# Two prompt tiles and the samples are routed first, and the V products of four tiles are made in one pass

## What is computed

```python
q = (x @ w_query).reshape(T, 8, 2, 128)
s = einsum('thpd,hpkd->thpk', q, sub_keys)           # 128 scores per head and side
s1, i1 = top_k(s[:, :, 0], 16); s2, i2 = top_k(s[:, :, 1], 16)
top_s, top_pos = top_k(all 256 sums s1[a] + s2[b], 16)
e_idx = (i1 * 128 + i2) at top_pos;  gate = softmax(top_s)
a = gelu(einsum('thkd,td->thk', u_tab[e_idx], x))    # exact gelu
y = einsum('thk,thkd->td', gate * a, v_tab[e_idx])
```

## Time and profile before

| | |
|---|---|
| median of 3 runs | 3245.22 us (3241.13 to 3252.75) |
| profiled execution | 3243.07 us, span 3241.0 us |
| PE busy | 3143.3 us, 97% of the span |
| PE weight load | 2775.6 us, 86% |
| DVE busy | 2379.3 us, 73% |
| ACT busy | 995.1 us, 31% |
| POOL busy | 796.9 us, 25% |
| mean granted TensorE clock | 0.985 of full speed |
| moved by DMA | 754.30 MB, mean 233 GB/s |

### The profile page before, as it was taken

How to read it: one execution, slowest core, us unless ns; L and a number is a source line. 1 busy time by engine, 2 the same in 40 slices (tenths; PEclk the granted TensorE clock), 3 DMA queues, 4 the chain that set the end, 5 groups by cost and what they waited for, 6 DMA issues and landing times. The chain is left out here.

```text
span 3241.0 us, 49377 instructions
## 1 busy us (share of the span) xinstructions
PE 3143.3 (97%) x17258; PEld 2775.6 (86%) x17258; DVE 2379.3 (73%) x5085; ACT 995.1 (31%) x1487; POOL 796.9 (25%) x588
## 2 busy tenths in 40 slices
PE   6999999799999999999999999999999999999999
PEld 4777777578999999999999999977888888888887
DVE  5676555445999768999577777648888888888886
ACT  4323333222222123444222222223333334333333
POOL 0000000001111100000376656534333333433330
PEclk9999999899999999999999999999999999999999
DMA  4111110222221223778999999989999999999993
GB/s 164 41 47 58 55 41 28 92 92 96 72 72 59 69 92 115 241 239 259 334 412 377 369 360 360 353 299 403 364 353 352 357 354 392 383 356 352 353 351 139
DMA packets 324580, 754.30 MB, mean 233 GB/s; under 512 B 22456, under 2 KB 154044, under 8 KB 323312
## 3 DMA queue, kind: packets, MB, share of 16 engines
q1 hardware_dynamic: 145024, 408.29, 34.6%
q0 software_dynamic: 79776, 290.00, 23.7%
q10 hardware_dynamic: 99664, 54.56, 5.7%
HBM read 637.82 MB, written 114.95 MB: 232 GB/s over the span
## 5 line engine op out<-in xcount | busy, mean ns | idle before, releaser
L1251 PE MATMUL u_p<-hn_hi,u_hi 128*128 128x384 f32 x2048 | 699.4, 342 | 7.4 <-PEq L1274 3.7
L1253 PE MATMUL u_p<-hn_hi,u_lo 128*128 128x384 f32 x2048 | 692.9, 338 | 0.0
L1252 PE MATMUL u_p<-hn_lo,u_hi 128*128 128x384 f32 x2048 | 692.6, 338 | 0.0
L1941 POOL DMA_INDIRECT y_ring<-in_peer_v,row_idx x248 | 367.5, 1482 | 624.8 <-DVE yt L2083 574.8
L1745 POOL DMA_INDIRECT s_ring<-in_peer_u,row_idx x264 | 334.8, 1268 | 620.2 <-DVE row_idx L1838 411.7
L1987 PE MATMUL y_p<-v_hi,w_hi 128*128 128x512 f32 x1536 | 474.5, 390 | 10.4 <-DVE w_lo L2074 10.4
L1989 PE MATMUL y_p<-v_lo,w_hi 128*128 128x512 f32 x1536 | 474.2, 390 | 0.0
L1992 PE MATMUL y_p<-v_hi,w_lo 128*128 128x512 f32 x1536 | 473.7, 390 | 0.0
L1251 PEld LDWEIGHTS u_p<-hn_hi,u_hi 128*128 128x128 f32 x2048 | 386.0, 188 | 9.4 <-issue 7.4
L1252 PEld LDWEIGHTS u_p<-hn_lo,u_hi 128*128 128x128 f32 x2048 | 386.2, 189 | 0.0
L1253 PEld LDWEIGHTS u_p<-hn_hi,u_lo 128*128 128x128 f32 x2048 | 386.1, 189 | 0.0
(11 more groups left out here) (350 smaller groups left out, 4694.4 us busy)
## 6 DMA issues: line engine op xcount, KB each, us to landing
u_raw<-in_peer_ut SPq DMA_DIRECT2D x128, 512.0 KB, 7.7
late<-in_peer_v SPq DMA_DIRECT2D x64, 1024.0 KB, 7.4
down_raw<-in_peer_v SPq DMA_DIRECT2D x64, 1024.0 KB, 7.2
act_scratch<-act_tile SPq DMA_DIRECT2D x128, 384.0 KB, 5.7
gate_scratch<-gbuf ACTq DMA_DIRECT2D x6, 4096.0 KB, 16.4
gate_scratch<-late ACTq DMA_DIRECT2D x6, 4096.0 KB, 20.8
late<-act_scratch SPq DMA_DIRECT2D x64, 384.0 KB, 8.6
late<-gate_scratch SPq DMA_DIRECT2D x64, 384.0 KB, 10.3
```

Source lines behind the costliest of these rows:

```text
L1251: mm(b, uh[:, s, k, :], hn_hi[:, k, t], start=(k == 0), stop=False)
L1252: mm(b, uh[:, s, k, :], hn_lo[:, k, t], start=False, stop=False)
L1253: last = mm(b, ul[:, s, k, :], hn_hi[:, k, t], start=False, stop=(k == ND - 1))
L1941: nc.gpsimd.indirect_dma_start(out=ring[:, n % RING, :], out_offset=None, in_=A["peer_v"], in_offset=bass.IndirectOffsetOnAxis(ap=idx[:, N ...
```

## The change

The expert layer gets this order:

1. **First search** (10 blocks): queries (264 columns) and search for tiles 6, 7 and the samples only, one block per head. The low parts of U are on POOL here alone.
2. **First decode** (4 blocks): those tiles. Row numbers are written to `idx` here.
3. **Second search** (88 blocks): 16 sections of 6 and 5 blocks. A section searches three of tiles 0 to 5 for one head (queries of 384 columns, made from a second load of `w_query`). Between the six parts of a search DVE makes a U low part and some dots or adds (`fill_of`): 264 dots in sections 0 to 8, 192 adds of V rows in sections 9 to 15. Sample activations now use two buffers (`hb`), and `yt` holds first the rows for the dots and, once the last dot is done, the rows that are added to.
4. **Second decode** (6 blocks): tiles 0 to 5. Tiles 4 and 5 are not transposed; their expert numbers go to `idx`, together with the place of their activation in `act_scratch`.
5. **Gates** for 8 sub-blocks (512 tokens) with 16 blocks, then 4 blocks alone.
6. **V** in one pass over tiles 0 to 3, 64 pairs of 48 products. Tiles 4 and 5 stay dense in U, but go by rows in V: their activations, one number for each (token, pick), are fetched from `act_scratch` by 256 indexed fetches (`pick`), and 320 rows are fetched and added in all, 64 left of tile 7 and 256 of tiles 4 and 5. How many adds DVE makes after a pair is set by `due`.

The search keeps 64 of the 256 sums, those that can be among the top 16 (`RECTS`), and the decode has nine small chained operations that turn such a position into the two ranks.

The diff, cut to its core:

```diff
-NV1 = 8
-TL = TG // 2
+TV = 4
+GV = NC - TV
+NG2 = GV * P - NG
+TL = TV
-E_TOPK, E_DECODE = 22, 10
+E_K1, E_D1, E_K2, E_D2 = 10, 4, 88, 6
+K2_ADDS = 192
...
+    RECTS = [(0, 1, TOPK, 0), (1, 3, 8, 16), (4, 4, 4, 40), (8, 8, 1, 56)]
+    NCAND = 64
...
+            NSEC = 2 * PH
+            SD = 9
+            FIRST_U = [E0 + 11 * (s // 2) + 6 * (s % 2) for s in range(NSEC + 1)]
+            JOBS = [NDOT * min(s, SD) // SD + K2_ADDS * max(s - SD, 0) // (NSEC - SD) for s in range(NSEC + 1)]
...
+                def sample_row(i):
+                    if i >= 2:
+                        pool.wait_ge(dot_done, NG + i - 1)
+                    elif i == 1:
+                        pool.wait_ge(dot_done, NK)
+                    nc.gpsimd.dma_start(hb[i % 2][:, :], hs_dram[NG + i:NG + i + 1, :].broadcast_to([P, D])
+                                        ).then_inc(hb_in[i % 2], 16)
...
+                    if s == SD - 1:
+                        sp.wait_ge(dot_done, NDOT)
+                        sp.dma_start(yt[:, :, :], x2_dram[DENSE:SEQ, :].rearrange("(t p) d -> p t d", p=P)).then_inc(xt_in, 16)
...
+                for s in range(NSEC):
+                    for i, e in enumerate(range(FIRST_U[s], FIRST_U[s + 1])):
+                        if s + 1 < NSEC and i == 3:
+                            chunk(s + 1)
+                        if s + 1 < NSEC and i == 4:
+                            scores(s + 1)
+                        tile_products(pe, e)
...
+                    def fill(i):
+                        e = FIRST_U[s] + i + 1
+                        if e <= FIRST_U[s + 1]:
+                            u_low(dve, nc.vector, e, e % 2)
+                        a, z = (JOBS[s] + (JOBS[s + 1] - JOBS[s]) * x // 6 for x in (i, i + 1))
+                        for n in range(a, z):
+                            if n < NDOT:
+                                dot(n)
+                            else:
+                                add(n - NDOT)
...
+    KEPT = NG - K2_ADDS
+    NADD = KEPT + NG2
+    FROM = [1, 18, 58]
+    DONE = [0, KEPT, NADD]
...
+        def due(n):
+            for x in range(2):
+                if n <= FROM[x + 1]:
+                    return DONE[x] + (DONE[x + 1] - DONE[x]) * max(n - FROM[x], 0) // (FROM[x + 1] - FROM[x])
+            return NADD
...
+            def pick(c):
+                nc.gpsimd.indirect_dma_start(
+                    out=picked[:, c:c + 1], out_offset=None, in_=acts,
+                    in_offset=bass.IndirectOffsetOnAxis(ap=idx[:, NU + NG2 + c:NU + NG2 + c + 1], axis=0)
+                ).then_inc(act_in[c // SUB], 16)
...
+            for n in range(RING, KEPT + RING):
+                for c in range(2):
+                    pick(2 * (n - RING) + c)
+                row(n)
+            for n in range(KEPT + RING, NADD):
+                c = 2 * KEPT + n - KEPT - RING
+                if c < NG2:
+                    pick(c)
+                row(n)
...
-            for g in range(2):
-                pair(g, 0, 0, first=True)
-                with pe.Fori(0, NP // 2 - 1) as i:
-                    pair(g, 2 * i + 1, 1)
-                    pair(g, 2 * i + 2, 0)
-                pair(g, NP - 1, 1, last=True)
+            pair(0, 0, first=True)
+            with pe.Fori(0, NP // 2 - 1) as i:
+                pair(2 * i + 1, 1)
+                pair(2 * i + 2, 0)
+            pair(NP - 1, 1, last=True)
...
+            for n in range(NP - SLOTS):
+                pair(n, n % SLOTS, n // SLOTS, fresh=(n == 0))
+                adds(n)
```

More of the change, by code:

```diff
@@ new lines, in query_low, with query @@
+    def query_low(dve, n):
+        dve.wait_ge(wqhi_done, n + 1)
+        nc.vector.tensor_tensor(wql[:, :, :], wq[:, :, :], wqh[:, :, :].bitcast(F32),
+                                ALU.subtract).then_inc(wqlo_done, 1)
+    def query(pe, n, b, side, t):
+        if n >= 2:
+            pe.wait_ge(q_out, n - 1)
+        d = slice(side * P, (side + 1) * P)
+        for k in range(ND):
+            nc.tensor.matmul(b, wqh[:, k, d], hn_hi[:, k, t], start=(k == 0), stop=False)
+            nc.tensor.matmul(b, wqh[:, k, d], hn_lo[:, k, t], start=False, stop=False)
+            last = nc.tensor.matmul(b, wql[:, k, d], hn_hi[:, k, t], start=False, stop=(k == ND - 1))
+        last.then_inc(q_done, 1)
@@ L1641, in _ @@
                         a_store(sp, e, p)
-            sp.wait_ge(saved[0], 16 * (NSUB // 2) + 16)
+            with sp.Fori(0, NJ) as j:
+                four(j)
+            for e in range(R0, R0 + 2):
+                tile_in(sp, e)
+            for s in range(2):
+                sp.wait_ge(saved[s], 16 * NJ + 16)
+            for s in range(2):
+                Pair(sem, s, late[:, s * SLOT:(s + 1) * SLOT]).load(sp, A, a_dram, g_dram, s)
+            for e in range(R0 + 2, NK):
+                tile_in(sp, e)
         @block.tensor
@@ L1693, in _ @@
                                  gbuf[s][:, :, :].rearrange("i (q e) t -> i q e t", e=2)).then_inc(saved[s], 16)
+            with act.Fori(0, NJ) as j:
+                two(j)
+            for e in range(R0, NK):
+                tile_out(act, e)
         @block.vector
@@ L1889, in down_phase @@
-def down_phase(nc, A, O, own, sb, ps, sem, x2_dram, g_dram, a_dram, ys, yt, idx, wt, late):
+                            u_low(dve, nc.vector, G0 + 4 * j + 2 * s + n // 4 + 1, (n // 4 + 1) % 2)
+            with dve.Fori(0, NJ) as j:
+                two(j)
+            for e in range(R0 + 1, NK):
+                u_low(dve, nc.vector, e, e % 2)
+def down_phase(nc, A, O, own, sb, ps, sem, x2_dram, g_dram, a_dram, ys, yt, idx, wt, gate_tok, late):
     N = TL * P
@@ L1946, in _ @@
+            for n in range(RING):
+                row(n)
+            for p in range(2):
+                pool.wait_ge(a_out[p], 16 * (NK // 2))
+            for n in range(RING, KEPT + RING):
[6 more added lines that the diff above has]
+                    pick(c)
+                row(n)
         @block.sync
@@ L1973, in _, with pair @@
             mm = nc.tensor.matmul
-            def pair(g, j, s, first=False, last=False):
-                n = NP * g + j
+            def pair(n, s, first=False, last=False):
                 pe.wait_ge(vlo_done, 2 * n + 2)
@@ new lines, in weights, with evacuate @@
+            def weights(t):
+                c = slice((t - TV) * NK, (t - TV + 1) * NK)
+                dve.wait_ge(x2_in, 16)
+                for i in range(c.start // SUB, c.stop // SUB):
+                    dve.wait_ge(act_in[i], 16 * SUB)
+                w = slice(NG + c.start, NG + c.stop)
+                v.tensor_tensor(wt[:, w], picked[:, c], gate_tok[:, w], ALU.mult).then_inc(wt_done, 1)
+                dve.wait_ge(wt_done, t - TV + 1)
+            def evacuate(t):
+                if t == 0:
+                    dve.wait_ge(x_in, 16)
+                dve.wait_ge(tile_done, t + 1)
@@ new lines, in _ @@
+            q = NQ - 1
+            pair(SLOTS * q, 0, q)
+            pair(SLOTS * q + 1, 1, q)
+            mean(slice(TL, NT), len(FIRST))
+            pair(SLOTS * q + 2, 2, q)
+            inverse(slice(TL, NT), 1)
+            pair(SLOTS * q + 3, 3, q)
+            for t in FIRST:
+                scale(t, 1)
+            for t in range(TL):
+                evacuate(t)
+                mean(slice(t, t + 1), len(FIRST) + t + 1)
+                inverse(slice(t, t + 1), t + 2)
+                scale(t, t + 2)
```

1123 lines of the change are left out of this document (550 added, 573 removed).

## The result

| | before | after |
|---|---|---|
| median of 4 runs | 3248.98 us (3241.13 to 3254.18) | 3290.26 us (3284.89 to 3301.98) |
| profiled execution | 3243.07 us | 3285.14 us, span 3283.3 |
| up to 742 us, the mixer | 742 | 742 |
| everything up to V | 1424 us | 1529 us |
| V with start and tail | 1075 us | 1012 us |

The ratio is 1.0127 with a 95% interval of 1.0101 to 1.0152: the kernel became **slower by 1.3%**. The forecast was faster by 0.7%; the measured time lies inside the range that it gave, 3115 to 3320, but on the other side of no change.

The account below looks back on a forecast made before the run. TensorE's products were taken to set the time now, busy 98 to 100% from 742 us on. 3243 + 86 for the stages before V - 108 for V = 3221 us, 3223 on the runs' scale; range 3115 to 3320.

Parts of the forecast that it names:

- First search, first decode, second decode and gates: Four stages before V, forecast at 150, 46, 71 and 237 us.
- The third part of V: Rows 200 to 319 of V: VectorE sets 2.14 us a row, 257 us, with DMA just carrying it at 399 GB/s.
- the prediction's own signs against it: In V: a pick under 0.6 us, GpSimd waiting for the ring early, or TensorE above 90% would disprove that part.
- the one for the second search: Second search: VectorE busy under 88% would prove its forecast of about 1000 us wrong.
- Rival (c): Late in V, DMA binds at 364 GB/s: a pair takes 15.0 us instead of 13.7, kernel 3247; chance 0.09.
- the price of a call in V: In V, GpSimd calls cost 1.36 and 1.42 us each: 192 calls take 261 us, 256 take 364.
- Rival (a): In V, GpSimd's calls cost more: at 1.6 us V takes 1059, the kernel 3313 + 2; chance 0.30.
- the mismatch term of the second search: Second search: VectorE waits 17 us where long TensorE stretches meet its short ones and the other way round.
- VectorE is the bound there: Second search: VectorE's work of 934 us against TensorE's 883, busy 93% or more, stage 1006 us with waits.
- the end of V: After V's last add: six pairs 65 us and tail 8.
- (b): In V, a pick is cheap, 0.7 us with its gap: V 801, the kernel 3055; chance 0.13.
- (d): Second search: fills hide VectorE's waits, so 1006 falls to some 935, the kernel to 3150; chance 0.06.

Follow-up runs that it names:

- a1: The changed kernel without V's 256 fetches of single activations (output differs): 3106.1 us, ratio 0.9546, V 824 us.
- a2: The changed kernel with each add of a fetched row in V on 16 of 1024 columns (output differs): 3257.5 us, ratio 1.0034.
- c2: The changed kernel with 256 instead of 192 adds in the second search and V's rows spread late: 3233.6 us, ratio 0.9937.
- d2: The changed kernel with VectorE in V waiting for four rows, so adds come in bursts of four: 3284.1 us, ratio 1.0106.
- d1: The changed kernel with the 88 low parts of U in the second search back on GpSimd: 3306.4 us, ratio 1.0187.
- b3: The changed kernel with dots and adds of the second search on 16 of 1024 columns (output differs): 3236.3 us, one run.
- b1: The changed kernel with each section's first low part of U ahead of the search's first maxima: 3269.9 us, ratio 1.0063.
- b2: The changed kernel with the eight sample dots spread, one after each 16 dots of tile 7: 3278.2 us, ratio 1.0085.
- c1: The changed kernel with V's adds respread: 64 until pair 24, 136 until pair 53, 120 in pairs 53 to 59: 3233.0 us, ratio 0.9944.
- e1: The three edits of c3 with a later spread: 64 adds until pair 25, 136 until 56, 120 beside 56 to 59: 3189.1 us, ratio 0.9823.
- c3: The changed kernel with the edits of b1, b2 and c1 together: 3200.0 us, ratio 0.9844.

## Why the prediction was wrong, step by step

**The change of stages was read rightly.** First search, first decode, second decode and gates came within 7 us each (147, 39, 75, 235 for 150, 46, 71, 237). Nothing of what TensorE saved on gates was left, as forecast, and V was set by GpSimd for two thirds, with no engine else full. The third part of V, 257 us for its last 120 rows, took 259. Of the prediction's own signs against it, none of those for V came and the one for the second search did, VectorE under 88% (83%). The rate at which DMA binds was right too: 397 GB/s for 259 us, where the earlier trace rows had 403 for 72 us. Rival (c) did not come. The Trainium skill's 358 GB/s per core (DMA: Bandwidth & Descriptors, Specifications) is below what a single working core moves here, and its page HBM Reference (Specifications) says so of a core streaming alone; a1's 406 GB/s for 462 us agrees.

**The step that failed is the price of a call in V**, "1.36 and 1.42 us a call, so 261 and 364 us". It is 275 / 192 = 1.43 and 378 / 256 = 1.48, 28 us more, of the 45 that V took above its sum. The prediction itself had put the point of no gain at 1.44, and had the row for 1.48, 27 calls in 40 us; it set it aside because VectorE would be less busy. VectorE was less busy (57 and 68% against 79%), but that is not what counts. Rival (a) was the right mechanism, at a smaller price than its 1.6. What a call costs hangs on the moment at which it starts. Three calls of the kernel after, and the adds beside them:

```profile
2608.78 1.08 POOL L2080 DMA_INDIRECT y_ring<-in_peer_v,row_idx  x1 [0.30 <-issue]
2610.17 0.94 POOL L2071 DMA_INDIRECT picked_act<-act_scratch,row_idx  x1 [0.30 <-issue]
2611.42 1.65 POOL L2080 DMA_INDIRECT y_ring<-in_peer_v,row_idx  x1 [0.30 <-issue]
```

```profile
2607.76 1.28 DVE L2225 SCALAR_TENSOR_TENSOR y_late<-y_ring,row_weight,y_late 128x1024 f32<-128x1024 f32 x1
2610.97 1.29 DVE L2225 SCALAR_TENSOR_TENSOR y_late<-y_ring,row_weight,y_late 128x1024 f32<-128x1024 f32 x1 [1.92 <-DMA y_ring<-in_peer_v,row_idx]
```

The first call starts when the add has 0.26 us to go and takes 1.08; the second meets none and takes 0.94; the third has 0.84 us of an add ahead of it and takes 1.65. In each the time is what is left of the add, plus 0.82, and never below 0.94. So it is for 413 of the 448 calls, to 0.07 us; nearly all of the others start as the instruction of VectorE begins, and take 0.94 where this would give 2.08. The 182 calls that start within no instruction of two SBUF inputs take 0.95 at most, though the DMA engines are busy for 82 and 83% there; the other 266 take 1.28 in the mean, and that lengthening is 89 us of the 653. All instructions of VectorE that lengthen a call here read two inputs in SBUF; no run sets one of the same length with one input beside the calls, so that it needs two is not shown. The pair's own low parts lengthen calls as well as adds do (a2, c2), and a VectorE that waits for rows makes short separate stretches, each of which can catch a call (d2). The Trainium skill (SBUF — State Buffer, Who interferes with whom) says that the ports which VectorE and GpSimd share are an exclusive lock, and that a VectorE instruction with two SBUF inputs contends with a GpSimd instruction that reads SBUF; the three calls agree. d1 shows it in the other direction, a dot of 3.18 us beside a low part on GpSimd.

**Second, the mismatch term of the second search**, "17 where TensorE's long stretch (a query chunk beside an expert, 16.8) meets a short one of VectorE". VectorE's waits for high parts of U and of the query are 73.0 + 12.1 = 85 us. The other waits were well sized: 10.8 + 15.0 + 6.8 + 13.9 = 46.5 for 9 + 21 + 9 + 16 = 55. With its waits of 131.6 taken off, VectorE's work, with the short gaps between its instructions, is 901 us where the sum had 934, so the forecast had 33 too much work and 60 too little waiting, together the 27. The claim that VectorE is the bound there, at 93%, is wrong as a claim about one engine: with dots and adds of 16 columns (b3), the search still lasts 975. The bound is a chain of two engines with one block of slack; order alone is worth 30 us (b1), the samples' dots 12 (b2) and load 52 for 64 adds (c2).

**Third, the end of V**, 65 + 8 = 73 us for six pairs and the tail. From 3197 us on it was 86: 6 until the weights of the next pair are there, 67 for six pairs (the first, behind a stop of TensorE, took 12.7, the others 10.9), 13 for tile sums, roots and stores. The first eight rows took 14 for 12, and with the 2 of the third part that is V's 45: 2 + 28 + 2 + 13.

Together: -3 - 7 + 27 + 4 - 2 + 45 = 64, and 3221 + 64 = 3285, the profiled execution. The forecast's margin was 22 us; the price of the calls alone used it up, the other two made the kernel slower.

**The rivals that failed.** (b), a cheap call for 4 bytes: its duration is that of 4 KB, 0.94 us. (d), fills that hide VectorE's waits: 132 us of waits stayed, and the search took 1033 us where (d) had some 935.

**What the prediction did not see.** It took the spread of adds over pairs (`due`) as given. With calls as the bound, the pairs beside them are free for TensorE up to its 10.9 us each. The change puts 39 pairs under 653 us of calls and leaves 25 for the stretches where DMA and VectorE are full or nothing is beside them. With 52 there (c1) V falls by 56 us: the sign of the change hangs on a schedule. TensorE's clock says where that time lay: 0.82 of full speed over the 378 us in which TensorE was busy for 70%, a mean between its levels of 1.2 and 2.4 GHz. In e1's second part, with TensorE busy for 87% of it, it is 0.93.

**Still open.** How much of V's gap to the 697 us of TensorE could be had is not shown. Fewer calls for the same picks would be the way; none that does it was tried. In the search, c3 stands 100 us above TensorE's sum of 896, of which load, order, start and end are shown as causes. In its trace TensorE waits 48 us for low parts, and 28 pass between the last product of U and the next stage; what each cause has of the 48 is not shown.

## What to carry to other kernels

Count an engine's calls, not their bytes: an indexed fetch of 4 bytes costs GpSimd what one of 4 KB does, and if the calls set a stage, add to the price what is left, on average, of VectorE's two-input instruction when a call starts, or take it from the busiest row that you have. Where a stage is set by one engine's fixed count of calls, put as much of the other engines' work beside them as will fit, and only then judge the change. Where two engines hand each other work with a slack of one block, neither's sum of busy time is the stage: look for what stands ahead of the handed-over instruction in its engine's order.

## What was not expected of the hardware

- VectorE and GpSimd hold each other up in both directions, and not only at row fetches. A GpSimd call that starts within `v_lo` or `w_lo` takes up to 1.97 us instead of 0.94. A dot that starts within a GpSimd subtraction takes 3.18 instead of 1.23. In d1, giving the low parts to a GpSimd that was busy for 56% made VectorE busy for 69 us more, though it had 107 us less to do.
- With VectorE still for 28 us, 23 calls were issued in c2, 1.22 us each, and in that kernel's first 160 us, VectorE busy for 38%, 1.50. Between these ends the price is set by how many calls start within a two-input instruction and how much of it is left, not by VectorE's busy share as such.

```profile
2512.00:2540.00 28.00, 0.00 (x0) 0.00 (x0) 0.00 (x0) 0.00 (x0) 21.12 (x23) 0.50 0.02 0
```

- The 16 DMA engines stayed at 397 to 406 GB/s for 259 and 462 us, with fetched rows of 4 KB in over half of the bytes. In a2 that pace held a stage in which no compute engine but TensorE was above half.
